# Prompt attention in four rounds: one program, projections between tiles, normalised probabilities, values as weights

## The chip, the cores and the metric

One core of a Trainium2 chip runs the whole program. The metric is the device time of one execution in microseconds (us). The engines are TensorE (PE in the profile, its weight loads PEld), VectorE (DVE), ScalarE (ACT), GpSimd (POOL) and SyncE (SP, which issues most DMAs). Each works through its own list of instructions in order; semaphores join them.

## What is computed

One step of a two-layer decoder. In each layer three mixers work on the same input: latent attention, a short convolution, and a recurrent mixer. The change concerns the attention of the 1024 prompt tokens, with 8 heads. In the reference:

```python
s = (jnp.einsum('bqhc,bkc->bhqk', q_lat, ckv).astype(jnp.float32)
     + jnp.einsum('bqhr,bkr->bhqk', q_pe, kpe).astype(jnp.float32)) * ATTN_SCALE
mask = k_pos[None, :] <= q_pos[:, None]
s = jnp.where(mask[None, None], s, -jnp.inf)
p = jax.nn.softmax(s, axis=-1).astype(ckv.dtype)
...
o_mla = jnp.einsum('bthc,chv->bthv', o_lat, p['w_uv']).reshape(B, T, D_MLA)
y_mla = (o_mla * jax.nn.silu(z_mla)) @ p['w_mla_out']
```

`q_lat` is the non-rotary part of the query (64 numbers a head) taken through `w_uk`, `q_pe` its rotary part (32 numbers), `ckv` the latent of 256 numbers a token. The kernel computes keys (ckv through w_uk) and values (ckv through w_uv) of each head instead, which gives the same sums. Everything is float32.

## The kernel before

`attention` (L2287 on) runs, for each layer, `prompt_attention` inside a hardware loop over four pairs of heads (the rounds), then the decoding stages for 64 sample tokens. Each call of `prompt_attention` is a phase: at its end the semaphores are cleared and all engines meet.

A round has three parts.

Projections. SP loads the round's columns of w_q_b in three pieces a head (L1756 to L1758), w_uk and w_uv. PE computes the queries of two heads in six groups of up to 364 tokens (L1770), ACT copies them to `q_t` (L1864), DVE applies the rotary factors to rows 64 to 95 of each head (L1902, L1903, L1905). PE computes keys (L1775; ACT copies, L1868) and values (L1779; DVE copies, L1908), turns w_uk (L1786) and computes the latent queries of the samples (L1795). POOL copies the rotary keys below the others (L1893).

Tiles. A tile is one block of 128 queries (`qt`, 0 to 7) of one head; it sees `(qt + 1) * 128` keys. The order is head by head: eight tiles of head 0, then eight of head 1. For each tile: scores on PE (L1808) into one of two banks of 1024 columns; on DVE the causal mask on the last 128 columns (L1919), the maximum (L1921) and its negative (L1923); on ACT the exponential with its row sum (L1884); on PE the transposes of the 128x128 blocks (L1817), on ACT their copies to `probs_t` (L1857); on PE the outputs, with the turned probabilities as 128-column weights and 64 columns of values streaming (L1827); on DVE the reciprocal of the sum (L1928) and the scaling of the 128x64 output (L1931).

End. The 128x128 results of the eight query blocks, two heads beside each other, are turned (L1846), and DVE multiplies them into `o_mla`, which holds the gate (L1944).

What sets the order of the work on PE is written out by hand:

```python
for a in range(n_jobs + 1):
    if a < n_jobs:
        pe.wait_ge(exped, a + 1)
        for f in range(len(fours[a])):
            turns(a, f)
    if a + 2 < n_jobs:
        scores(a + 2)
    if a:
        for f in range(len(fours[a - 1])):
            outputs(a - 1, f)
```

ACT does in turn the exponential of tile a and the copies of tile a - 1; DVE the maximum of tile a + 2 and the scaling of tile a - 1.

Two other places are named later. `page_attention` (the decoding stage) computes the values of two halves of a group in turn, with 64 columns of weights and output rows 0 to 63 or 64 to 127 (L2138), between transposes of full width (L2124) and scores (L2114). L723 is in the convolution.

## Time and profile before

| | |
|---|---|
| runs shown | 4146.57, 4148.21, 4152.67 us; median 4148.21 |
| the profiled execution | 4152.63 us, span of its instructions 4150.2 us |
| mean granted TensorE clock | 0.92 of full speed |
| PE busy | 3670.6 us (88% of the span), 28472 matmul instructions |
| PE weight loads busy | 2433.3 us (59%) |
| DVE busy | 1620.1 us (39%) |
| ACT busy | 888.2 us (21%) |
| POOL busy | 263.3 us (6%) |
| largest groups | L842 (gates, 787.9 us), L498 (projections), L2114, L2138, L2408 |

Busy times of PE are modelled ends of pipelined matmuls and overlap; a share of the whole span is a mean over stages with different limits. Prompt attention lies at about 1160 to 1468 us in layer 0 and 3195 to 3502 us in layer 1.

### The profile page before, as it was taken

To read this page: it belongs to the slowest core of one execution; us is meant where nothing else is said; L and a number is where in the kernel's file an instruction comes from. 1 tells how busy PE (TensorE), PEld (TensorE's weight loads), DVE (VectorE), ACT (ScalarE), POOL (GpSimd) and SP (SyncE) were. 2 spreads that over 40 slices of the span, in tenths; PEclk is the share of its full clock that TensorE was granted. 3 is DMA by queue.
4 is the path that set the end of the run, shared out by engine and by line. 5 is a ranking of instruction groups with operands and counts; after the bars stand their busy time and mean duration, and the time that the engine had idled before them with its cause. 6 is when DMAs were issued, how large, how long until landed. Compare 5 with 4: busy or idle time off the path is not lost. (4 is left out here: it accounts for less than half of the span.)

```text
span 4150.2 us, 67196 instructions
## 1 busy us (share of the span) xinstructions
PE 3670.6 (88%) x28472; PEld 2433.3 (59%) x28472; DVE 1620.1 (39%) x3054; ACT 888.2 (21%) x1778; POOL 263.3 (6%) x285
## 2 busy tenths in 40 slices
PE   5989989999778879989979899899995888899996
PEld 3555656666456657755536555566663665676654
DVE  3021024544344558844122010344433444777422
ACT  1110012222133422221022000222211443222201
POOL 0000000000000024400000000000000000442000
PEclk9999989999688979989979999999995998899998
DMA  7210111111000047734251110211110000775433
GB/s 269 51 38 16 46 43 53 50 51 54 13 18 7 6 166 271 274 115 138 74 192 25 51 33 16 64 47 53 56 41 16 7 6 7 275 263 202 149 119 121
DMA packets 282621, 362.89 MB, mean 87 GB/s; under 512 B 57188, under 2 KB 234294, under 8 KB 265832
## 3 DMA queue, kind: packets, MB, share of 16 engines
q1 hardware_dynamic: 244640, 190.00, 15.3%
q0 software_dynamic: 25808, 155.47, 10.1%
q10 hardware_dynamic: 11896, 13.44, 0.9%
q8 instruction: 210, 3.44, 0.3%
q14 instruction: 67, 0.55, 0.0%
HBM read 310.50 MB, written 48.35 MB: 86 GB/s over the span
## 5 line engine op out<-in xcount | busy, mean ns | idle before, releaser
L842 PE MATMUL rwkv_gate_bank<-u,rwkv_gate_w 128*128 128x364 f32 (+1 forms) x2304 | 787.9, 485 | 8.7 <-DMA rwkv_wa<-in_rwkv_a_dram 8.7
L842 PEld LDWEIGHTS rwkv_gate_bank<-u,rwkv_gate_w 128*128 128x128 f32 x2304 | 421.1, 192 | 232.1 <-issue 11.1
L498 PE MATMUL mla_b<-u,mla_w 128*128 128x364 f32 (+1 forms) x960 | 297.7, 473 | 27.6 <-DMA mla_w<-in_w_in_dram 27.6
L2173 DVE STREAM_TRANSPOSE u<-dec_ckv 128x2048 f32<-128x2048 f32 x112 | 258.5, 2308 | 52.9 <-DMA dec_ckv<-in_cache_mla_ckv_dram,dec_page_row 52.9
L2114 PE MATMUL dec_s_bank<-u,att_q_rows 32*64 32x256 f32 x8192 | 244.6, 386 | 32.6 <-DVE kpe L2176 32.6
L498 PE MATMUL rwp_b<-u,rwp_w 128*128 128x364 f32 (+1 forms) x864 | 267.0, 473 | 3.6 <-DMA rwp_w<-in_w_in_dram 3.6
L498 PEld LDWEIGHTS mla_b<-u,mla_w 128*128 128x128 f32 x960 | 184.7, 193 | 139.0 <-DMA mla_w<-in_w_in_dram 27.8
L2408 PE MATMUL out_b<-merged,out_w 128*128 128x364 f32 (+1 forms) x768 | 239.9, 477 | 13.0 <-DMA out_w<-in_w_out_dram 13.0
L498 PE MATMUL conv_b<-u,conv_w 128*128 128x364 f32 (+1 forms) x768 | 238.8, 475 | 4.9 <-DMA conv_w<-in_w_in_dram 4.9
L2138 PE MATMUL dec_o_bank<-dec_ckv,cq 128*64 128x256 f32 x1792 | 234.9, 382 | 7.7 <-DVE att_o_all L2199 6.5
L2114 PEld LDWEIGHTS dec_s_bank<-u,att_q_rows 32*64 32x64 f32 x8192 | 185.8, 135 | 74.4 <-DVE kpe L2176 39.8
L498 PEld LDWEIGHTS rwp_b<-u,rwp_w 128*128 128x128 f32 x864 | 166.0, 192 | 103.6 <-DMA rwp_w<-in_w_in_dram 3.8
L2408 PEld LDWEIGHTS out_b<-merged,out_w 128*128 128x128 f32 x768 | 148.8, 194 | 104.1 <-DMA out_w<-in_w_out_dram 14.2
L1893 POOL COPY attn_k_t<-kpe 32x1024 f32<-32x1024 f32 x16 | 16.1, 1032 | 3036.7 <-POOLq L171 3036.7
L856 ACT ACTIVATE rwkv_gate_stage<-rwkv_gate_bank 128x364 f32<-128x364 f32 x144 | 67.7, 470 | 648.2 <-PE rwkv_gate_bank L842 647.6
L498 PEld LDWEIGHTS conv_b<-u,conv_w 128*128 128x128 f32 x768 | 148.3, 193 | 94.5 <-DMA conv_w<-in_w_in_dram 5.1
L2138 PEld LDWEIGHTS dec_o_bank<-dec_ckv,cq 128*64 128x64 f32 x1792 | 145.8, 137 | 87.8 <-issue 32.7
L1808 PE MATMUL attn_s<-attn_k_t,attn_q_t 96*128 96x512 f32 (+3 forms) x384 | 160.9, 534 | 6.8 <-ACT att_q_lat L1876 6.8
L1827 PEld LDWEIGHTS attn_b<-attn_v,attn_probs_t 128*128 128x128 f32 x1152 | 146.9, 194 | 27.4 <-issue 19.7
L1770 PE MATMUL attn_s<-cq,attn_wq 128*128 128x364 f32 (+1 forms) x288 | 106.7, 537 | 62.4 <-DMA attn_wq<-in_w_q_b_dram 62.4
L2157 ACT ACTIVATE ckv<-dec_s_bank,dec_minus_top 128x1024 f32<-128x1024 f32 x64 | 71.3, 1114 | 370.7 <-DVE dec_minus_top L2185 370.7
L1827 PE MATMUL attn_b<-attn_v,attn_probs_t 128*128 128x64 f32 x1152 | 143.3, 271 | 0.0
(470 smaller groups left out, 4716.7 us busy)
## 6 DMA issues: line engine op xcount, KB each, us to landing
merge_sig<-gates_feature_major SPq DMA_DIRECT2D x16, 1632.0 KB, 8.8
mod_w<-in_w_ada_dram SPq DMA_DIRECT2D x12, 2048.0 KB, 13.6
rwkv_gate_w<-in_w_in_dram SPq DMA_DIRECT2D x48, 512.0 KB, 4.0
gates_feature_major<-rwkv_gate_stage SPq DMA_DIRECT2D x96, 182.0 KB, 1.9
mla_w<-in_w_in_dram SPq DMA_DIRECT2D x18, 512.0 KB, 3.8
rwp_w<-in_w_in_dram SPq DMA_DIRECT2D x18, 512.0 KB, 4.0
u<-x_feature_major SPq DMA_DIRECT2D x8, 1088.0 KB, 14.3
out_x<-x_feature_major SPq DMA_DIRECT2D x16, 544.0 KB, 4.3
```

The source lines that it names most:

```text
L498: mm = pe.matmul(self.banks[j % len(self.banks)][:, 0:m], self.w[:, n % self.NW, k, :], s.u[:, k, t0:t0 + m], start=(k == 0), stop=(k == K ...
L842: mm = pe.matmul(self.banks[j % 2][:, 0:m], self.w[:, n % GATE_CHUNKS, k, :], self.s.u[:, k, t0:t0 + m], start=(k == 0), stop=(k == KD - 1))
L856: act.activation(self.stage[j % 3][:, 0:m], self.banks[j % 2][:, 0:m], ACT.Copy).then_inc(self.emptied, 1)
L1770: mm = pe.matmul(B01[j % 2][:, 0:m], wq[:, k, i, :], s.cq[:, k, t0:t0 + m], start=(k == 0), stop=(k == 2))
L1808: mm = pe.matmul(B01[a % 2][:, c:c + n], q_t[i][0:QK, qt * P:(qt + 1) * P], k_t[i][0:QK, c:c + n], start=True, stop=True)
L1827: mm = pe.matmul(out_b[a % 2][:, 0:VH], probs_t[:, j % 4, x * P:(x + 1) * P], v[:, kt, i * VH:(i + 1) * VH], start=(kt == 0), stop=(kt == qt))
L1893: pool.tensor_copy(k_t[i][64:96, :], s.kpe[64:96, 0:SEQ]).then_inc(kpe_copied, 1)
L2114: mm = pe.matmul(S[64 * half:64 * half + NQ, 512 * i:512 * i + NK], q, keys, start=(cb == 0), stop=(cb == BLOCKS))
L2138: mm = pe.matmul(O[64 * half:64 * half + NQ, 0:KV_LORA], probs_t[:, j * P + 64 * half:j * P + 64 * half + NQ], ckv[(2 * a + half) % NS][:, ...
L2157: act.activation(probs.rearrange("p (j i k) -> p i j k", j=KEYS, i=4), s_view.rearrange("p i (j k) -> p i j k", j=KEYS), ACT.Exp, scale=AT ...
L2173: dve.transpose(kt[o % NT].rearrange("p (c j k) -> p j c k", c=BLOCKS, j=KEYS), ckv[o % NS].rearrange("p (j c k) -> p j c k", c=BLOCKS, j= ...
L2408: mm = pe.matmul(banks[j % NB][:, 0:m], w[:, n % NW, k, :], merged[:, k, t0:t0 + m], start=(k == 0), stop=(k == KD - 1))
```

## The change

`prompt_attention` is called once a layer, without the loop. It runs 64 tiles in one phase, `(round, query block, head)`, so that the two heads of a round alternate. The first round's projections stand ahead of the tiles; those of round r + 1 are cut into twelve pieces, which stand behind tiles 0 to 9 of round r (two each behind tiles 0 and 1). All projections and all transposed blocks go through one ring of two banks, written by PE and emptied by ACT; so ACT now copies the values too. Weights, keys, queries and values are doubled; the queries and keys lie in `s.u`, which is free in this stage. The rotary operations of the next round stand one by one behind tiles 3 to 10 on DVE.

DVE now divides by the row sum before the transposes: it scales the probabilities, up to 128x1024, in place (L1956 of the changed kernel). The outputs are computed once for both heads of a query block, two tiles later (L1845): 64 columns of values are the weights, 128 columns of turned probabilities stream, head 0 writes partitions 0 to 63 and head 1 partitions 64 to 127 of the same bank. The result is already turned: the transposes of L1846 go, and DVE multiplies 512 columns into `o_mla` (L1962) after each four query blocks.

```diff
-    NT = SEQ // P
+def prompt_attention(nc, s, l, q_lat, q_pe):
...
+    NT, NP = SEQ // P, HEADS // 2
...
-    tiles = [(i, qt) for i in range(2) for qt in range(NT)]
-    n_jobs = len(tiles)
-    fours = [[range(k, min(k + 4, qt + 1)) for k in range(0, qt + 1, 4)] for _, qt in tiles]
-    before = [sum(len(f) for f in fours[:a]) for a in range(n_jobs + 1)]
+    tiles = [(r, qt, i) for r in range(NP) for qt in range(NT) for i in range(2)]
+    qg = [(i, g) for i in range(2) for g in range(NG)]
+    pieces = [("q", x) for x in range(6)] + [("k", 0), ("k", 1), ("v", 0), ("v", 1), ("uk", 0), ("lat", 0)]
+    after_tile = {0: 2, 1: 2, 2: 1, 3: 1, 4: 1, 5: 1, 6: 1, 7: 1, 8: 1, 9: 1}
+    blocks = lambda a: [range(k, min(k + 4, tiles[a][1] + 1)) for k in range(0, tiles[a][1] + 1, 4)]
+
+    ring, pieces_at = [(0, *p) for p in pieces], {}
+    for a, (r, qt, i) in enumerate(tiles):
+        ring += [("turn", a, f) for f in range(len(blocks(a)))]
+        first = sum(after_tile.get(x, 0) for x in range(a % 16))
+        pieces_at[a] = [(r + 1, *p) for p in pieces[first:first + after_tile.get(a % 16, 0)]] if r + 1 < NP else []
+        ring += pieces_at[a]
+    slot = {job: j for j, job in enumerate(ring)}
...
-        wq = ph.sb("wq", [P, 3, 2, P])
-        wuk, wuv = ph.sb("wuk", [P, 2, P]), ph.sb("wuv", [P, 2, P])
+        wq = [ph.sb(f"wq{i}", [P, 3, 2, P]) for i in range(2)]
...
-        q_t = [ph.sb(f"q_t{i}", [P, T]) for i in range(2)]
-        k_t = [ph.sb(f"k_t{i}", [P, SEQ]) for i in range(2)]
+        q_t = [[s.u[:, 2 * x + i, :] for i in range(2)] for x in range(2)]
+        k_t = [[s.u[:, 4 + 2 * x + i, 0:SEQ] for i in range(2)] for x in range(2)]
...
-        v = ph.sb("v", [P, NT, P])
-        probs = ph.sb("probs", [P, 2, SEQ])
-        probs_t = ph.sb("probs_t", [P, 4, 512])
...
-        o = ph.sb("o", [P, NT, P])
-        B = [ph.bank(f"s{i}", (P, 1024)) for i in range(2)] + [ph.bank(f"b{i}") for i in range(4)]
-        B01, turn, out_b = B[0:2], B[2:4], B[4:6]
...
+        S = [ph.bank(f"s{i}", (P, 1024)) for i in range(2)]
+        R = [ph.bank(f"ring{i}") for i in range(2)]
+        O = [ph.bank(f"o{i}") for i in range(2)]
...
+                for r in range(NP):
+                    x = r % 2
+                    if r >= 2:
+                        sp.wait_ge(ring_written, slot[(r - 2, "lat", 0)] + 1)
...
+                def ring_bank(job):
+                    j = slot[job]
                     if j >= 2:
-                        pe.wait_ge(q_read, j - 1)
-                    for k in range(3):
...
-                def turns(a, f):
-                    j = before[a] + f
-                    if j >= 2:
-                        pe.wait_ge(copied, j - 1)
-                    for x, kt in enumerate(fours[a][f]):
-                        mm = pe.transpose(turn[j % 2][:, x * P:(x + 1) * P], probs[:, a % 2, kt * P:(kt + 1) * P], s.tab["ident"])
-                    mm.then_inc(turned, 1)
-
-                def outputs(a, f):
-                    i, qt = tiles[a]
-                    j = before[a] + f
-                    pe.wait_ge(copied, j + 1)
-                    if f == 0 and a >= 2:
-                        pe.wait_ge(read, a - 1)
-                    for x, kt in enumerate(fours[a][f]):
-                        mm = pe.matmul(out_b[a % 2][:, 0:VH], probs_t[:, j % 4, x * P:(x + 1) * P],
-                                       v[:, kt, i * VH:(i + 1) * VH], start=(kt == 0), stop=(kt == qt))
+                def turns(a):
+                    pe.wait_ge(normed, a + 1)
+                    for f, four in enumerate(blocks(a)):
+                        bank = ring_bank(("turn", a, f))
+                        for x, kt in enumerate(four):
+                            mm = pe.transpose(bank[:, x * P:(x + 1) * P], probs[a % 2][:, kt * P:(kt + 1) * P], ident)
+                        mm.then_inc(ring_written, 1)
+
+                def outputs(a):
+                    r, qt, _ = tiles[a]
+                    pair = a // 2
+                    if qt == 0:
+                        pe.wait_ge(ring_read, slot[(r, "v", 1)] + 1)
+                    if qt % 4 == 0 and pair >= NT:
+                        pe.wait_ge(evicted, 2 * (pair // NT - 1) + qt // 4 + 1)
+                    pe.wait_ge(ring_read, slot[("turn", a + 1, len(blocks(a + 1)) - 1)] + 1)
+                    for kt in range(qt + 1):
+                        for i in range(2):
+                            mm = pe.matmul(O[qt // 4][VH * i:VH * (i + 1), qt % 4 * P:(qt % 4 + 1) * P], v[r % 2][:, kt, VH * i:VH * (i + 1)],
+                                           probs_t[:, pair % 2, i, kt * P:(kt + 1) * P], start=(kt == 0), stop=(kt == qt))
                     mm.then_inc(summed, 1)
...
+                for p in pieces:
+                    prologue(0, *p)
                 scores(0)
                 scores(1)
...
+                for a in range(len(tiles)):
+                    turns(a)
+                    if a + 2 < len(tiles):
                         scores(a + 2)
-                    if a:
-                        for f in range(len(fours[a - 1])):
-                            outputs(a - 1, f)
...
+                    if a >= 2 and a % 2 == 0:
+                        outputs(a - 2)
+                    for p in pieces_at[a]:
+                        prologue(*p)
+                outputs(len(tiles) - 2)
...
+                def exponential(a):
+                    n = (tiles[a][1] + 1) * P
                     act.wait_ge(topped, a + 1)
                     if a >= 2:
...
+                        act.wait_ge(ring_written, slot[("turn", a - 2, len(blocks(a - 2)) - 1)] + 1)
+                    act.activation(probs[a % 2][:, 0:n], S[a % 2][:, 0:n], ACT.Exp, scale=ATTN_SCALE,
                                    bias=minus_top[:, a:a + 1], accum_out=total[:, a:a + 1]).then_inc(exped, 1)
-                    if a:
-                        copies(act, a - 1)
-                copies(act, n_jobs - 1)
+
+                def keep_turned(a):
+                    _, qt, i = tiles[a]
+                    for f, four in enumerate(blocks(a)):
+                        j = slot[("turn", a, f)]
+                        n = len(four) * P
+                        act.wait_ge(ring_written, j + 1)
+                        act.activation(probs_t[:, a // 2 % 2, i, 4 * f * P:4 * f * P + n], R[j % 2][:, 0:n], ACT.Copy).then_inc(ring_read, 1)
+
+                for p in pieces:
+                    keep(0, *p)
+                exponential(0)
+                for a in range(len(tiles)):
+                    if a + 1 < len(tiles):
+                        exponential(a + 1)
+                    keep_turned(a)
+                    for p in pieces_at[a]:
+                        keep(*p)
...
+                def rope(r, step):
+                    i, n = divmod(step, 4)
+                    q = q_t[r % 2][i]
+                    if n == 0:
+                        dve.wait_ge(ring_read, slot[(r, "q", 3 * i + 2)] + 1)
+                        if r or i:
+                            dve.wait_ge(roped, 6 * r + 3 * i)
+                        dve.tensor_tensor(swapped[64:96, :], q[96:128, :], sin, ALU.mult).then_inc(roped, 1)
+                    elif n == 1:
+                        dve.tensor_tensor(q[64:96, :], q[64:96, :], cos, ALU.mult).then_inc(roped, 1)
+                    elif n == 2:
+                        dve.wait_ge(roped, 6 * r + 3 * i + 2)
+                        dve.tensor_tensor(q[64:96, :], q[64:96, :], swapped[64:96, :], ALU.add).then_inc(roped, 1)
+                    else:
+                        dve.wait_ge(roped, 6 * r + 3 * i + 3)
+                        dve.tensor_copy(q_pe[64:96, :, 2 * r + i, :], q[64:96, SEQ:T].rearrange("p (b t) -> p b t", t=STEPS)).then_inc(q_pe_kept, 1)
...
-                def finish(a):
-                    i, qt = tiles[a]
+                def normalise(a):
+                    n = (tiles[a][1] + 1) * P
                     dve.wait_ge(exped, a + 1)
                     dve.reciprocal(inv_total[:, a:a + 1], total[:, a:a + 1]).then_inc(inverted, 1)
                     dve.wait_ge(inverted, a + 1)
-                    dve.wait_ge(summed, before[a + 1])
-                    dve.tensor_scalar(o[:, qt, i * VH:(i + 1) * VH], out_b[a % 2][:, 0:VH],
-                                      inv_total[:, a:a + 1], None, ALU.mult).then_inc(read, 1)
-
+                    dve.tensor_scalar(probs[a % 2][:, 0:n], probs[a % 2][:, 0:n], inv_total[:, a:a + 1], None, ALU.mult).then_inc(normed, 1)
+
+                def evict(n):
+                    r, h = divmod(n, 2)
+                    dve.wait_ge(summed, 8 * r + 4 * h + 4)
+                    out = s.o_mla[:, r, 512 * h:512 * (h + 1)]
+                    dve.tensor_tensor(out, out, O[h][:], ALU.mult).then_inc(evicted, 1)
...
+                for step in range(8):
+                    rope(0, step)
                 tops(0)
                 tops(1)
-                for a in range(n_jobs + 1):
-                    if a + 2 < n_jobs:
+                for a in range(len(tiles)):
+                    r, qt, i = tiles[a]
+                    normalise(a)
+                    if a + 2 < len(tiles):
                         tops(a + 2)
-                    if a:
...
+                    if r + 1 < NP and 3 <= a % 16 < 11:
+                        rope(r + 1, a % 16 - 3)
+                    if a % 16 == 9:
+                        evict(2 * r)
+                    elif r and a % 16 == 1:
+                        evict(2 * r - 1)
+                evict(2 * NP - 1)
...
-        with nc.Fori(0, HEADS // 2) as hp:
-            prompt_attention(nc, s, l, hp, q_lat, q_pe)
+        prompt_attention(nc, s, l, q_lat, q_pe)
```

How PE's instructions move: from tile 2's transposes on, before (`attn_s` holds scores, `attn_b` are the banks of transposes and outputs; the first number of the shape is the columns of weights or rows of output, the last the columns streamed):

```order
L1817 MATMUL attn_b<-tables,attn_probs 128x128 x3
L1808 MATMUL attn_s<-attn_k_t,attn_q_t 128x512
L1808 MATMUL attn_s<-attn_k_t,attn_q_t 128x128
L1827 MATMUL attn_b<-attn_v,attn_probs_t 128x64 x2
L1817 MATMUL attn_b<-tables,attn_probs 128x128 x4
L1808 MATMUL attn_s<-attn_k_t,attn_q_t 128x512
L1808 MATMUL attn_s<-attn_k_t,attn_q_t 128x256
L1827 MATMUL attn_b<-attn_v,attn_probs_t 128x64 x3
```

The same engine, tiles 4 and 5 of the first round, changed (`attn_ring` is the ring, `u` holds queries and keys, `attn_o` the output banks):

```order
L1832 MATMUL attn_ring<-tables,attn_probs 128x128 x3
L1823 MATMUL attn_s<-u 128x512
L1845 MATMUL attn_o<-attn_probs_t,attn_v 64x128 x4
L1792 MATMUL attn_ring<-ckv,attn_wuk 128x512 x2
L1832 MATMUL attn_ring<-tables,attn_probs 128x128 x3
L1823 MATMUL attn_s<-u 128x512
L1792 MATMUL attn_ring<-ckv,attn_wuk 128x512 x2
L1832 MATMUL attn_ring<-tables,attn_probs 128x128 x4
```

Outputs now come every second tile, for both heads, and the keys' projections of the next round (L1792) stand between the tiles.

On DVE, one tile before:

```order
L1928 RECIPROCAL attn_inv_total<-attn_total 128x1
L1931 TENSOR_SCALAR attn_o<-attn_b,attn_inv_total 128x64
L1919 TENSOR_TENSOR attn_s<-attn_s,tables 128x128
L1921 TENSOR_REDUCE attn_top<-attn_s 128x1
L1923 TENSOR_SCALAR attn_minus_top<-attn_top 128x1
```

And changed, tile 9 of the first round and what follows up to tile 10's scaling:

```order
L1954 RECIPROCAL attn_inv_total<-attn_total 128x1
L1956 TENSOR_SCALAR attn_probs<-attn_probs,attn_inv_total 128x640
L1945 TENSOR_TENSOR attn_s<-attn_s,tables 128x128
L1947 TENSOR_REDUCE attn_top<-attn_s 128x1
L1949 TENSOR_SCALAR attn_minus_top<-attn_top 128x1
L1936 TENSOR_TENSOR u<-u,attn_swapped 32x1088
L1962 TENSOR_TENSOR o_mla<-o_mla,attn_o 128x512
L1954 RECIPROCAL attn_inv_total<-attn_total 128x1
L1956 TENSOR_SCALAR attn_probs<-attn_probs,attn_inv_total 128x768
```

The scaling now stands ahead of the transposes and is 640 columns wide here instead of 64; a rotary operation and the product stand ahead of the next tile's scaling.

## Rows read from the trace of the kernel before

**Rows 1.** Windows by stage; window, length, busy us of each engine, clock, DMA, GB/s

```profile
1166.70:1189.60 22.90, 21.40 (x88) 14.21 (x88) 9.37 (x10) 6.37 (x15) 0.00 (x0) 0.93 0.09 20
1189.60:1234.70 45.10, 42.64 (x265) 33.47 (x265) 24.86 (x80) 22.75 (x56) 0.00 (x0) 0.92 0.00 1
1234.70:1242.50 7.80, 1.08 (x8) 0.84 (x8) 1.28 (x2) 1.28 (x1) 2.02 (x2) 0.73 0.17 30
1239.39:1315.59 76.20, 65.51 (x360) 48.44 (x360) 35.52 (x92) 30.41 (x73) 2.00 (x3) 0.90 0.04 9
1166.70:1465.50 298.80, 261.89 (x1440) 194.38 (x1440) 142.06 (x368) 120.34 (x287) 6.05 (x6) 0.91 0.04 8
3201.00:3499.90 298.90, 261.81 (x1440) 194.35 (x1440) 142.10 (x368) 120.34 (x287) 6.05 (x6) 0.91 0.04 8
```

**Rows 2.** Windows, in the first tiles and at the second round's first projections

```profile
1192.00:1194.00 2.00, 2.00 (x5) 1.06 (x5) 0.66 (x2) 0.59 (x3) 0.00 (x0) 0.50 0.00 0
1243.00:1247.00 4.00, 4.00 (x8) 2.11 (x8) 0.00 (x0) 0.40 (x1) 0.00 (x0) 0.50 0.37 82
```

**Rows 3.** Timeline across a round's end; start us, us, engine, line, [idle before <-releaser]

```profile
1235.49 1.28 DVE L1944 TENSOR_TENSOR o_mla<-o_mla,attn_b 128x512 f32 x2 [0.86 <-PE attn_b L1846]
...
1239.39 0.38 SPq L1756 DMA_DIRECT2D attn_wq<-in_w_q_b_dram  x1
...
1242.55 0.98 PE L1770 MATMUL attn_s<-cq,attn_wq 128*128 128x364 f32 x1 [6.78 <-DMA attn_wq<-in_w_q_b_dram]
```

**Rows 4.** Timeline of the first round: runs of equal instructions on PE and PEld

```profile
1169.91 9.08 PEld L1770 LDWEIGHTS attn_s<-cq,attn_wq 128*128 128x128 f32 x30 [0.27 <-issue]
1182.84 3.73 PE L1779 MATMUL attn_b<-attn_wuv,ckv 128*128 128x128 f32 x32
1187.69 1.10 PE L1795 MATMUL attn_b<-attn_q_t,attn_wuk_t 64*128 64x64 f32 x8 [0.68 <-ACT attn_wuk_t L1871]
1204.13 1.88 PE L1808 MATMUL attn_s<-attn_k_t,attn_q_t 96*128 96x512 f32 x4
1206.91 0.93 PE L1817 MATMUL attn_b<-tables,attn_probs 128*128 128x128 f32 x7
1230.67 3.43 PEld L1827 LDWEIGHTS attn_b<-attn_v,attn_probs_t 128*128 128x128 f32 x30
```

**Rows 5.** Timeline, the chain of the first 1024-column tile and the start of the next, of 128 columns

```profile
1206.05 0.30 DVE L1919 TENSOR_TENSOR attn_s<-attn_s,tables 128x128 f32<-128x128 f32 x1 [1.22 <-PE attn_s L1808]
1206.38 1.23 DVE L1921 TENSOR_REDUCE attn_top<-attn_s 128x1 f32<-128x1024 f32 x1
1207.83 1.11 ACT L1884 ACTIVATE attn_probs<-attn_s,attn_minus_top 128x1024 f32<-128x1024 f32 x1 [1.50 <-DVE attn_minus_top L1923]
1208.61 0.29 DVE L1921 TENSOR_REDUCE attn_top<-attn_s 128x1 f32<-128x128 f32 x1
1209.00 0.15 DVE L1928 RECIPROCAL attn_inv_total<-attn_total 128x1 f32<-128x1 f32 x1
1209.79 0.38 ACT L1884 ACTIVATE attn_probs<-attn_s,attn_minus_top 128x128 f32<-128x128 f32 x1
```

**Rows 6.** Groups by line and form: count, busy us, mean ns, idle before

```profile
L723 DVE TENSOR_SCALAR conv_y<-conv_past_p,vecs 128x1024 f32<-128x1024 f32 x4 | 2.8, 748 | 0.0
L723 DVE TENSOR_SCALAR conv_y<-conv_past_s,vecs 128x64 f32<-128x64 f32 x4 | 0.8, 249 | 0.0
L1902 DVE TENSOR_TENSOR attn_swapped<-attn_q_t,tables 32x1088 f32<-32x1088 f32 x16 | 20.6, 1287 | 134.8 <-ACT attn_q_t L1864 134.8
L1944 DVE TENSOR_TENSOR o_mla<-o_mla,attn_b 128x512 f32 x16 | 10.3, 683 | 6.9 <-PE attn_b L1846 6.9
```

**Rows 7.** Timeline in the decoding stage, PE: halves side by side, then full-width transposes

```profile
1707.36 3.67 PE L2138 MATMUL dec_o_bank<-dec_ckv,cq 128*64 128x256 f32 x32
1710.96 1.09 PE L2124 MATMUL dec_pt_bank<-tables,ckv 128*128 128x128 f32 x8
1711.98 3.71 PE L2114 MATMUL dec_s_bank<-u,att_q_rows 32*64 32x256 f32 x128
```

208 lines of the change are left out of this document (86 added, 122 removed).

## The prediction

> **What bounds the kernel now.** I read the windows by stage first, because the change touches one stage only, prompt attention, which runs once in each of the two layers. From the first projection matmul to the last product it takes 298.8 us in the first layer and 298.9 us in the second [rows 1], together 598 of 4150 us. Nothing else in the program is edited, so the sum is made over these two stretches. Look at two things in rows 1. PE is busy for 262 of 298.8 us, while DVE has 142 and ACT 120: TensorE is the bound, and a change of DVE or ACT work is worth nothing unless it ends up in TensorE's way. And the four rounds repeat: a round is 76.2 us, of which the projections take 22.9 us, the 16 tiles 45.1 us and the gap between rounds 7.8 us with 1 us of PE work in it.
>
> Next the granted clock: it is 0.50, that is 1.2 GHz, in the first microseconds of the tiles, behind a stretch in which PE mostly waited, and again at the start of the next round's projections behind the gap [rows 2]. So a gap costs twice, once as idle time and once as slow matmuls after it.
>
> Then the timeline across the end of a round, to see what the 7.8 us are: the last products on DVE, the end of the phase (semaphores cleared, all engines meet), and then PE idle for 6.8 us until the weights have come, whose first load SP issues only at 1239.39 [rows 3].
>
> Last the pace of TensorE's instructions at full clock [rows 4]. The "busy" durations overlap, so I divide the length of a run of equal instructions by their number. Each float32 matmul stands twice in the profile. Projection of 364 columns: 9.08/30 = 0.303 us each. Values, 128 columns: 3.73/32 = 0.117. Scores: (1.88 - 0.17)/4 = 0.427 for 512 columns, where 0.17 is the tail of the last one, so 0.834 ns a column; the keys have the same form. Transposes, one instruction each: about 0.115. The probability-times-value matmuls (L1827) stream only 64 columns, yet take 3.43/30 = 0.114: they go at the pace of their 128-column weight loads.
>
> **The sum, round by round, before.** Projections: 36 x 0.303 = 10.9, keys 8 x 0.427 = 3.4, values 32 x 0.117 = 3.7, the turned w_uk and the sample latents 1.6 (the latter 1.1 in rows 4): 19.6 us. Scores: 9216 columns, twice, x 0.834 ns = 15.4. Transposes 72 x 0.115 = 8.3. Outputs 144 x 0.114 = 16.4. The eight transposes of the result 0.9. That is 60.6 of 76.2 us; the other 15.6 us are the gap (6.8), slow clock, and waits at the seams and between small tiles.
>
> **Part 1, one program of four rounds.** The loop and three of four phase ends go. The weights of the next round are loaded a round ahead, so SP's DMA issues no longer stand before PE. Gone per layer: three gaps of 7.8 us and the slow projections after them. The first round's 22.9 us [rows 1] stay, and I add 0.5 us since all its results now pass through two banks and ACT takes the values' copies as well.
>
> **Part 2, projections between tiles.** They are not hidden: PE is the bound, so their 19.6 us are paid in full. What they fill are the waits of the small tiles. ACT, busy for 30 of 76 us a round [rows 1], takes 1.4 us of values' copies more and stays hidden. The rotary work on DVE is not quite: three operations of 1.29 us for each head [rows 6], one behind each of tiles 3, 4, 5, 7, 8 and 9. DVE then has for tile 8 (768 columns reduced, 640 scaled): mask 0.33, reduce 0.96 (between 0.29 for 128 and 1.23 for 1024, rows 5), two small ones 0.30, multiply 0.55, rotary 1.29, together 3.4 us, and for tile 9 a product of 0.68 more [rows 6], 4.1 us. PE has 0.6 of transposes, 1.3 of scores, 0.6 of outputs and 0.45 of w_uk: 2.9 us. I take 3 us a round of waiting for DVE; bounds are 0 (the slack of two tiles absorbs it) and 7.7 (all six operations in PE's way).
>
> **Part 3, normalised probabilities.** Was: 128x64 scaled after the output. Now: the reciprocal and a multiply over up to 1024 columns stand before the transposes. No such multiply of attn_probs exists yet; the nearest, DVE TENSOR_SCALAR from and to SBUF by a per-row number, takes 748 ns at 1024 columns and 249 ns at 64 [rows 6], so 0.22 + 0.52n/1000, some 8 us of DVE a round, where DVE had 35.5 of 76. The chain that matters is from the end of a tile's scores to its transposes. For 1024 columns: the scores' streaming ends at about 1205.84; mask at 1206.05, reduce 1.23, exponential 1.11, reciprocal at 1209.00 [rows 5]; plus 0.15, the multiply 0.75 and a hop of 0.1: 4.2 us. PE has between the two, by the new order, one outputs call, the other tile's transposes and scores: 1.9 + 0.3 + 0.9 + 1.7 = 4.8 us. Hidden, by 0.6 us. For 128 columns the reduce and the exponential fall to 0.29 and 0.38 [rows 5] and the multiply to about 0.3, so the chain is 2.0 us, while PE has 0.9 us: a hole of 1.1 us per pair, then about 0.9, 0.6 and 0.4 for 256, 384 and 512 columns, 3 us together. In rounds 1 to 3 the pieces fill these; in the last round nothing does.
>
> **Part 4, values as weights, two heads side by side.** The 144 outputs now load 64 columns of weights and stream 128 columns; the two heads write partitions 0 to 63 and 64 to 127 of one bank, in turn. The trace of before has this form in the decoding stage with 256 columns: 32 instructions in 3.67 us [rows 7], 0.113 us each, where 256 columns alone would take 256 x 0.834 = 0.213. So two halves do run at once. For 128 columns the bounds are 0.053 (half of 107 ns) and 0.115 (no overlap, like L1827). I take 0.06, since rows 7 stand 6 ns above half: 144 x 0.06 = 8.6 us instead of 16.4. The result comes out turned already, so 0.9 us of transposes go.
>
> Against this stands the change of shape. Behind the halves the next eight full-width transposes take 1.02 us from their first start to the start of what follows (1710.96 to 1711.98), 0.128 each instead of 0.107 to 0.115 [rows 7], 0.1 to 0.17 us for a change. There are two changes per outputs call, 16 a round: at 0.16, 2.6 us a round, 21 us over both layers; bounds 0 and 0.3. The Trainium skill (TensorEngine Tiling (Array Packing), Key Properties) says that changing the tiling mode, unlike changing only the tile, drains TensorE. It is the rule against this change; by rows 7 the drain is short, and without it the forecast would be 21 us lower.
>
> **Sum per layer.** A round with next projections: 19.6 + 15.4 + 8.3 + 8.6 + 2.6 = 54.5, plus 3 = 57.5 us, three times: 172.5. Last round: 34.9 + 3 of holes + 2.8 at its end (the last tile's normalising is exposed by 1.4, then copy and product) = 40.7. First projections 23.4. Slow clock in the first tiles, as in rows 2, and once more in the thin tiles of the last round: 5. Total 241.6, against 298.8: 57.2 less, 114.5 for both layers. The profiled execution took 4152.6 us around its span of 4150.2; the median of the runs shown is 4148.2, 4.4 lower. On the median: **4034 us**. A measurement of this kernel can tell about 0.2% (8 us) from no change.
>
> **The rivals.**
> *A. The heads do not overlap at 128 columns*, because the weight loads of both halves share one path. For it: L1827 shows loads setting the pace. Against: rows 7. Outputs then cost 0.115: 7.9 us more a round, of which some 2 were waiting anyway: 24 a layer, **4082**.
> *B. DVE binds.* The rotary operations are all in the way (7.7 instead of 3) and PE waits some 2 us a round more at the two ring banks while ACT copies keys (two copies of 0.6 us). 7 us in three rounds, 21 a layer: **4076**. For it: DVE is in order and each tile needs it twice. Against: its work is some 38 us in 57 (35.5 now [rows 1], less the 128x64 scalings and the values' copies, about 6, plus 8).
> *C. Slower: weights exposed.* Inside each head's strip the load cannot go under the running matmul and the strips take turns: 0.11 + 0.115 = 0.225 an instruction, 24 us more a round. Less the 8 us of waits that this covers, 87 a layer against 57 gained: 60 us slower, **4208**. It turns the sign from 0.173 us an instruction on (65/576 above 0.06). Rows 7 show 0.113 for twice the columns, so this is unlikely.
> That the change does not do what it says can only mean that the gaps stay inside the tiles; that is B.
>
> **How the numbers follow.** Forecast 0.64, A 0.17, B 0.14, C 0.03, anything else 0.02. The low bounds together (0.053, no change of shape, no DVE waits, no slow clock) are 28 us a layer, 3977; all at once is unlikely, so the range starts at 3995 and ends above A, at 4090. Faster 0.96, same 0.01, slower 0.03.
>
> **What would show it.** In the changed profile: each stretch near 242 us; no PE gap of several us inside it; L1845 at 0.055 to 0.07 us an instruction (A: 0.11); TensorE's clock at full level from the second round on; DVE as releaser of the transposes for a few us a round (B: over 7). The sum is wrong if PE's idle time in the tiles grows, or if L1832 and L1823 after L1845 start more than 0.3 us late.

## The result: 1.9% slower

The changed kernel takes **4228.7 us** (median of 4 runs, 4224.8 to 4233.6) against 4149.7 us of the kernel before (4 runs). The ratio is **1.0191, 95% interval 1.0173 to 1.0209**: slower by 79 us, where 114 us less was forecast. It lies above the range of 3995 to 4090.

### The profile after

First the stage in whole, by windows: the two stretches from the first projection matmul to the last product on DVE, then, of layer 0, the first projections and the four rounds, cut where the first transpose of each starts. The columns are those of [rows 1].

```profile
1167.60:1504.70 337.10, 254.15 (x1408) 162.39 (x1408) 154.72 (x360) 123.70 (x285) 0.00 (x0) 0.89 0.03 7
3238.00:3580.10 342.10, 261.71 (x1408) 166.58 (x1408) 154.76 (x360) 123.93 (x285) 0.00 (x0) 0.86 0.03 7
1167.60:1190.00 22.40, 21.53 (x88) 14.29 (x88) 8.07 (x8) 6.87 (x13) 0.00 (x0) 0.91 0.18 41
1192.90:1272.70 79.80, 59.72 (x320) 38.21 (x320) 38.22 (x89) 30.25 (x71) 0.00 (x0) 0.92 0.07 15
1272.70:1352.90 80.20, 61.79 (x352) 39.22 (x352) 38.82 (x90) 30.41 (x72) 0.00 (x0) 0.91 0.00 1
1352.90:1433.00 80.10, 60.96 (x352) 39.42 (x352) 38.80 (x90) 30.13 (x72) 0.00 (x0) 0.91 0.00 1
1433.00:1504.70 71.70, 49.40 (x292) 30.74 (x292) 28.96 (x76) 23.51 (x54) 0.00 (x0) 0.79 0.00 1
```

The stretches are 337.1 and 342.1 us against 298.8 and 298.9 [rows 1]: 38.3 + 43.2 = 81.5 us more, which covers the whole difference of 79 us. PE has less work than before, and in the first layer it is busy for 254 us, not 262; but it now stands idle for 83 us of the stretch, not 37. Two things are striking. The first projections take 22.4 us, about as forecast. And a round takes 80 us, more than before, gap and all, and the last one 71.7 us, although it has no next projections in it and 19.6 us less work on PE: a round's length no longer follows PE's work. (Part of the 71.7 us is the clock, which is lower in the last round, 0.79 against 0.91.)

Next who waits for whom, in layer 0 (1167 to 1505 us): us in total, times, longest. Then the two groups of the whole page in which those waits stand.

```profile
DVE attn_s L1945 <- PE attn_s L1823: 156.9, 63, 5.2
PEld attn_ring L1832 <- DVE attn_probs L1956: 102.6, 48, 3.5
PE attn_ring L1832 <- DVE attn_probs L1956: 80.4, 47, 3.3
ACT attn_probs L1893 <- DVE attn_minus_top L1949: 73.5, 32, 4.4
...
PE attn_o L1845 <- ACT attn_probs_t L1902: 0.7, 1, 0.7
```

```profile
L1832 PE MATMUL attn_ring<-tables,attn_probs 128*128 128x128 f32 x576 | 103.1, 313 | 158.5 <-DVE attn_probs L1956 158.3
L1945 DVE TENSOR_TENSOR attn_s<-attn_s,tables 128x128 f32<-128x128 f32 x128 | 38.3, 299 | 318.2 <-PE attn_s L1823 318.2
```

Read the first and third line together. PE's transposes (L1832) wait for DVE's scaling 80.4 us, in 47 of 64 tiles. And DVE's mask (L1945), the head of the maximum, waits for PE's scores 156.9 us, in 63 of 64. Neither engine is full, and each waits for the other about once a tile. That is the sign of a loop. The tiles without such a wait on PE are 1, 2, 3, 7 and 15 of the first three rounds and 1 and 15 of the last; in tiles 1, 2, 3 and 7 PE has projections of the next round to do meanwhile. PE's wait for ACT, which empties the ring of two banks, is 0.7 us in the tiles (last line), so the ring is not what holds it up.

The timeline shows one lap of it (start us, us, engine, line; in brackets the idle time before and who ended it):

```profile
1254.00 1.01 ACT L1893 ACTIVATE attn_probs<-attn_s,attn_minus_top 128x896 f32<-128x896 f32 x1 [2.50 <-DVE attn_minus_top L1949]
...
1254.82 0.98 PE L1832 MATMUL attn_ring<-tables,attn_probs 128*128 128x128 f32 x7 [2.50 <-DVE attn_probs L1956]
...
1255.64 1.88 PE L1823 MATMUL attn_s<-u 96*128 96x512 f32 x4
...
1257.45 1.53 PE L1845 MATMUL attn_o<-attn_probs_t,attn_v 128*64 128x128 f32 x24
1257.56 0.30 DVE L1945 TENSOR_TENSOR attn_s<-attn_s,tables 128x128 f32<-128x128 f32 x1 [2.80 <-PE attn_s L1823]
1257.89 1.22 DVE L1947 TENSOR_REDUCE attn_top<-attn_s 128x1 f32<-128x1024 f32 x1
1259.15 0.15 DVE L1949 TENSOR_SCALAR attn_minus_top<-attn_top 128x1 f32<-128x1 f32 x1
1259.22 0.15 DVE L1954 RECIPROCAL attn_inv_total<-attn_total 128x1 f32<-128x1 f32 x1
1259.34 1.12 ACT L1893 ACTIVATE attn_probs<-attn_s,attn_minus_top 128x1024 f32<-128x1024 f32 x1 [2.85 <-DVE attn_minus_top L1949]
1259.41 0.69 DVE L1956 TENSOR_SCALAR attn_probs<-attn_probs,attn_inv_total 128x896 f32<-128x896 f32 x1
1260.15 0.98 PE L1832 MATMUL attn_ring<-tables,attn_probs 128*128 128x128 f32 x7 [1.17 <-DVE attn_probs L1956]
...
1265.55 1.09 PE L1832 MATMUL attn_ring<-tables,attn_probs 128*128 128x128 f32 x8 [2.70 <-DVE attn_probs L1956]
```

From the transposes of one tile (12) to those of the next (13), at 1254.82 and 1260.15: transposes 0.82, scores 1.92, mask 0.33, maximum 1.26, its negative 0.07, reciprocal 0.19, scaling 0.74, together **5.33 us, and one tile further**. Nothing in it overlaps anything else in it. PE's own work in the same lap is 0.8 + 1.9 + 1.3 = 4.0 us, and in the laps of odd tiles, without outputs, 2.7. A round of 80 us is 16 laps of 5.0 us in the mean, the last one 16 of 4.5. (The last line above is the transposes of tile 14; they are used further down.)

**Theory L (the loop).** DVE does in order: scale a, find the maximum of a + 2, scale a + 1. PE does in order: transposes of a, scores of a + 2. So scale a → transposes a → scores a + 2 → maximum a + 2 → scale a + 1. The last step is no need of the data: the exponential of a + 1 was ready long before (in the lap shown it ended at 1255.01, its reciprocal started at 1259.22). It is DVE's list alone that puts scaling a + 1 behind a maximum whose scores wait for scaling a. In the kernel before the transposes waited for the exponential only; the way round (exponential a → transposes a → scores a + 2 → maximum a + 2 → exponential a + 2) led two tiles on.

**Rivals.** N: the DVE work of the scaling itself is too much (any order would be slow). D: DVE binds through the rotary operations (B of the prediction). O: the outputs side by side, or what is around them, cost more than was thought (A and C of the prediction).

### The profile page after: what moved, and what is told of

It is laid out like the page before. It is cut to its first block and busy times, and to the rows that moved or that the text cites. A ratio compares the mean times of both kernels' runs of the same rounds, so it can differ in the third digit from the quotient of the medians.

```text
span 4227.1 us, 66254 instructions
## 1 busy us (share of the span) xinstructions
PE 3652.9 (86%) x28408; PEld 2364.3 (56%) x28408; DVE 1644.5 (39%) x3038; ACT 892.4 (21%) x1772; POOL 255.1 (6%) x277
## 5 line engine op out<-in xcount | busy, mean ns | idle before, releaser
L1832 PE MATMUL attn_ring<-tables,attn_probs 128*128 128x128 f32 x576 | 103.1, 313 | 158.5 <-DVE attn_probs L1956 158.3
L1832 PEld LDWEIGHTS attn_ring<-tables,attn_probs 128*128 128x128 f32 x576 | 72.2, 157 | 209.3 <-DVE attn_probs L1956 203.2
L1823 PE MATMUL attn_s<-u 96*128 96x512 f32 (+3 forms) x384 | 176.2, 575 | 0.0
L2125 POOL DMA_INDIRECT dec_ckv<-in_cache_mla_ckv_dram,dec_page_row x112 | 105.8, 944 | 999.0 <-DVE dec_page_row L2237 733.4
L1945 DVE TENSOR_TENSOR attn_s<-attn_s,tables 128x128 f32<-128x128 f32 x128 | 38.3, 299 | 318.2 <-PE attn_s L1823 318.2
```

Source lines behind the costliest of these rows:

```text
L1823: mm = pe.matmul(S[a % 2][:, c:c + n], q_t[r % 2][i][0:QK, qt * P:(qt + 1) * P], k_t[r % 2][i][0:QK, c:c + n], start=True, stop=True)
L1832: mm = pe.transpose(bank[:, x * P:(x + 1) * P], probs[a % 2][:, kt * P:(kt + 1) * P], ident)
L1945: dve.tensor_tensor(d, d, s.tab["causal"], ALU.add).then_inc(masked, 1)
L2125: pool.indirect_dma_start(ckv[o % NS], None, ckv_rows, rows).then_inc(c_in[o % NS], 16)
```

## The experiments

The kernels were run in three groups of four (e1 to e4, e5 to e8, e9 to e12), each beside runs of the kernel before. That takes 4146.8 us (7 runs) in the first group, 4432.4 (10 runs) in the second and 4150.2 (15 runs) in the third. The 285 us more of the second group lie outside prompt attention, as far as the traces of e7 and e8 can tell (last section), so its kernels are compared by their difference to before and by the length of the stretch; the times expected of them were worked out from 4150 us and are read the same way.

### e1: scores ahead of transposes

```diff
                 for a in range(len(tiles)):
-                    turns(a)
                     if a + 2 < len(tiles):
                         scores(a + 2)
+                    turns(a)
```

> PE issues the scores of tile a+2 ahead of the transposes of tile a; nothing else changes. Theory L (a loop of one tile: scaling of a, transposes of a, scores of a+2, maximum of a+2, scaling of a+1, because DVE and PE work in order): the scores leave the loop, a lap spans two tiles, and PE binds again in the large tiles. PE's waits for the scaling fall from 158 us to under 50, the time to 4040 to 4080 us. Theory D (DVE has too much work, above all the rotary operations): DVE's work is the same, so the time stays at 4210 to 4230. Theory C (the chain from the scores' end to the transposes, 4 to 5 us, is too long for two tiles in flight): a part comes back, as the scores start earlier, 4150 to 4190.

Measured: 4044.5 us (4041.4 to 4050.8), ratio **0.9743 [0.9727, 0.9759]**. Two lines swapped on PE turn 79 us of loss into 102 us of gain. The windows of rounds 0 to 2 and the whole stretch:

```profile
1190.00:1248.00 58.00, 53.27 (x291) 33.89 (x292) 38.39 (x92) 30.20 (x72) 0.00 (x0) 0.97 0.11 23
1248.00:1306.00 58.00, 55.02 (x348) 35.96 (x345) 37.77 (x88) 29.35 (x71) 0.00 (x0) 1.00 0.00 1
1306.00:1364.00 58.00, 55.47 (x351) 36.24 (x349) 37.74 (x89) 29.12 (x70) 0.00 (x0) 1.00 0.00 1
1166.90:1413.00 246.10, 227.45 (x1408) 148.71 (x1408) 153.39 (x360) 122.17 (x285) 0.00 (x0) 0.98 0.05 10
```

The windows are 58 us long and PE is busy for 55 of them from the second on; counted from first transpose to first transpose (1251.25, 1310.09, 1368.93) a round is 58.8 us. TensorE's clock is at full level from the second round on. DVE does the same 153 us of work as in the changed kernel (154.7): the work was never the trouble. In place of 80.4 us the transposes wait 11.9 us for the scaling in layer 0:

```profile
PE attn_ring L1832 <- DVE attn_probs L1956: 11.9, 15, 1.9
```

### e2: no scaling

The multiplication of the probabilities by the reciprocal is left out (the output is not normalised), and the transposes wait for the exponential. PE's and DVE's orders are those of the changed kernel.

```diff
-                    pe.wait_ge(normed, a + 1)
+                    pe.wait_ge(exped, a + 1)
...
-                    dve.wait_ge(inverted, a + 1)
-                    dve.tensor_scalar(probs[a % 2][:, 0:n], ...).then_inc(normed, 1)
```

> The multiplication of the probabilities by the reciprocal of their sum is left out; the transposes wait for the exponential alone. Theory L: DVE's scaling no longer releases the transposes, the loop is gone: 4020 to 4060 us. Theory D: only the 66 us of multiplications over both layers go, at most: 4165 or more. Theory C: the chain is shorter by the multiplication, the reciprocal and their hops, about 1 us in each of 64 laps of two tiles, about 4150.

Measured: 4020.3 us, ratio 0.969 [0.9673, 0.9706]. Against 1.0191 the scaling in its place costs 5 points; against e1 (0.9743) it costs half a point. So it is its place in the loop that costs, hardly its time. (e1 and e2 differ in PE's order too; e12 finds that order worth 0.1% in the kernel before.)

### e3: scaling ahead of the maximum

```diff
                 tops(1)
+                normalise(0)
                 for a in range(len(tiles)):
...
-                    normalise(a)
+                    if a + 1 < len(tiles):
+                        normalise(a + 1)
                     if a + 2 < len(tiles):
                         tops(a + 2)
```

> DVE does the scaling of tile a+1 ahead of the maximum of tile a+2 instead of behind it. Theory L: the loop is cut at another place, but DVE now waits for the exponential between a maximum and the scaling of the same tile (1.3 us of 4.1 a large tile, partly under the rotary operations): 4060 to 4110 us. Theory D: no change, 4210 to 4230. Theory C: no change or slower, since DVE stands still for the exponential.

Measured: 4053.9 us, ratio 0.9765 [0.9749, 0.9781], some 6 us better than the lower end expected. PE's order is that of the changed kernel here, transposes first; only DVE's list is changed. That the loop opens from either side is the strongest sign for L: a cost of TensorE (O) would not go by an edit of DVE's list, and all of DVE's work (N) is still there.

### e4: the heads one after the other

e1, with the outputs of head 0 all ahead of those of head 1, in place of one of each in turn.

```diff
-                    for kt in range(qt + 1):
-                        for i in range(2):
+                    for i in range(2):
+                        for kt in range(qt + 1):
```

> As e1_scores_first, but the outputs of head 0 all stand before those of head 1, so the two halves of the array no longer alternate. If TensorE binds after e1, this adds (0.107 - 0.055) x 1152 = 60 us, or 30 to 60 with waits absorbed. If another chain still binds in e1, it adds under 15 us. The instructions' own pace shows whether alternating is what makes the halves overlap: 0.11 us each against 0.055.

Measured: 4087.1 us, ratio 0.9849 [0.9833, 0.9866], 43 us more than e1, inside the 30 to 60 expected. The runs of equal outputs on PE, first in e1, then in e4:

```profile
1226.12 1.09 PE L1845 MATMUL attn_o<-attn_probs_t,attn_v 128*64 128x128 f32 x16
...
1239.71 0.98 PE L1832 MATMUL attn_ring<-tables,attn_probs 128*128 128x128 f32 x7
1240.62 1.53 PE L1845 MATMUL attn_o<-attn_probs_t,attn_v 128*64 128x128 f32 x24
1242.08 1.98 PE L1823 MATMUL attn_s<-u 96*128 96x512 f32 x4
```

```profile
1253.07 2.89 PE L1845 MATMUL attn_o<-attn_probs_t,attn_v 128*64 128x128 f32 x28
...
1257.99 3.33 PE L1845 MATMUL attn_o<-attn_probs_t,attn_v 128*64 128x128 f32 x32
```

In e1 eight more instructions take 1.53 - 1.09 = 0.44 us, **0.055 each**; in e4 four more take 3.33 - 2.89 = 0.44, **0.110 each**. The same instructions run at twice the pace if the halves alternate. 576 x 0.055 = 32 us a layer would be the full price; 43/2 = 22 show, the rest fell into waits. With O the changed kernel would owe its loss to these outputs; they run at 0.055 in it too (below).

### e5: the scaling alone, put into the kernel before

Nothing of the change but the scaling of the probabilities ahead of the transposes, in the changed kernel's order; the four phases a layer, the gaps and the outputs with 128-column weights stay.

```diff
-                        pe.wait_ge(exped, a + 1)
+                        pe.wait_ge(normed, a + 1)
...
-                for a in range(n_jobs + 1):
+                for a in range(n_jobs + 2):
+                    if a < n_jobs:
+                        normalise(a)
                     if a + 2 < n_jobs:
                         tops(a + 2)
-                    if a:
-                        finish(a - 1)
+                    if a >= 2:
+                        finish(a - 2)
```

`normalise` is that of the changed kernel, and `finish` only copies.

> The kernel before with one part of the change alone: DVE scales the probabilities by the reciprocal ahead of the transposes (which wait for it), and only copies the outputs, of tile a-2, behind the maximum of tile a+2. The loop of four rounds, the old order of tiles and the old outputs stay. Theory L: the same one-tile loop appears in the old kernel, 4 to 5.3 us for a large tile against some 3.5; the 16 tiles of a round go from 45 to 60 to 66 us: 4270 to 4320 us. Theory N (the scaling is harmful only together with the projections and rotary operations between the tiles): under 4190.

Measured: 4763.5 us against 4432.4, ratio **1.0738 [1.072, 1.0756]**: 331 us more, where 120 to 170 more than before were expected. Right in sign, but twice the size: the clock was left out. A window from the first projections to just before the last products of layer 0, the waits for the scaling in that layer, and one lap:

```profile
1167.40:1628.90 461.50, 364.39 (x1428) 268.66 (x1429) 166.15 (x429) 127.84 (x287) 6.05 (x6) 0.67 0.02 5
```

```profile
PE attn_b L1818 <- DVE attn_probs L1931: 69.8, 48, 1.8
```

```profile
1218.87 1.15 PE L1818 MATMUL attn_b<-tables,attn_probs 128*128 128x128 f32 x6 [1.72 <-DVE attn_probs L1931]
...
1219.81 3.35 PE L1809 MATMUL attn_s<-attn_k_t,attn_q_t 96*128 96x512 f32 x4
...
1225.92 1.57 PE L1818 MATMUL attn_b<-tables,attn_probs 128*128 128x128 f32 x7 [1.70 <-DVE attn_probs L1931]
```

The stretch ends at 1633.2 and is 465.8 us long, 167 more than the 298.8 of [rows 1]; twice that, 334, is the whole difference of 331 us. The lap is 7.05 us, and the granted clock is 0.67 of full speed over the stretch, against 0.91 before: four scores take 3.35 us instead of 1.88. The waits for the scaling are 69.8 us, and the stretch is 167 us longer, so the loop costs twice. PE waits in 48 of 64 tiles, the clock is lower, and since transposes and scores are part of the lap, the lap grows, with the wait still in it.

### e6: the same, scores first

e5 with `scores(a + 2)` ahead of the wait for `normed` and of the transposes.

> As e5_scaling_alone, with the scores of tile a+2 ahead of the transposes of tile a on PE. Theory L: the loop is gone, DVE's 66 us of extra work lie mostly beside PE's: 4150 to 4190 us. Theory N: no change against e5.

Measured: 4448.0 against 4432.4, ratio 1.0033 [1.0022, 1.0045]: 16 us more than before, where 0 to 40 were expected. The same edit as e1 takes 7 points off. It ran in the same group as e5, and its stretch is 307.4 us at a mean clock of 0.92 (e5: 0.67), so the low clock came with the loop.

```profile
1166.70:1474.10 307.40, 265.55 (x1440) 193.06 (x1440) 166.60 (x432) 125.22 (x287) 6.05 (x6) 0.92 0.04 8
```

What is left, 16 us, is what the scaling costs this kernel in a good order.

### e7, e8: rotary operations on POOL

e7 is the changed kernel, e8 is e1, each with the rotary multiplications, sums and copies on POOL in place of DVE (same operations, `pool.` for `dve.`).

> The changed kernel with all rotary operations and the copies of q_pe on POOL instead of DVE; the order of PE and DVE as in the changed kernel. Theory L: the six rotary operations of a round lie in the loop with their full 1.29 us, less where PE's projections are longer than the lap (tile 3): 3 rounds x 2 layers x 6 x 1.29 = 46 us at most come off, some is given back in the first round if POOL is slower: 4185 to 4205 us. The large rest of the loss stays. Theory D: DVE's load was the bound, so most of the loss goes: under 4130.

> Scores first (as e1) and the rotary operations on POOL. With the loop cut, PE binds (55 of 58 us a round busy), so taking 8 us a round off DVE brings little: 4020 to 4045 us, against 4044 for e1. If POOL's slower operations hold up the first round, up to 10 us are given back: to 4055.

Measured: e7 4469.4 us, ratio 1.0084 [1.0067, 1.0101], 37 us more than before, where L expected 35 to 55 (the changed kernel: 79); e8 4323.9 us, ratio 0.9757 [0.9741, 0.9774], 108 us less than before (e1: 102), also as expected. In the changed kernel the operations lengthened some of the laps, and taking them away gives back half of the loss (the stretches are 318 and 322 us instead of 337 and 342), but it stays slower than before. Theory D had expected it under the time of before. With the loop open nothing is to be had: e8's stretches are 247 and 245 us, e1's 246 and 246. So D is a part of what fills the lap, and not the cause. On POOL one of these takes 2.48 us, against 1.29 on DVE [rows 6]; there is room for it.

### e9, e10, e11: what e1 still leaves

e9 is e1 with e3's order on DVE. e10 is e1 with the outputs ahead of the transposes:

```diff
                         scores(a + 2)
-                    turns(a)
                     if a >= 2 and a % 2 == 0:
                         outputs(a - 2)
+                    turns(a)
```

e11 is both.

> The changed kernel with both orders mended: PE issues the scores of tile a + 2 ahead of the transposes of tile a (as in e1), and DVE scales tile a + 1 ahead of the maximum of tile a + 2 (as in e3). Theory L (one lap of PE, DVE and ACT for each tile): e1 has opened the lap already, and 23.8 us of waiting for the scaling are left in both layers together, most of it where rotary operations stand ahead of the scaling on DVE. With the second order the scaling no longer stands behind a maximum, so some of these go: 0 to 15 us less than e1, a ratio to before of 0.970 to 0.975 (e1: 0.9743). Rival (the two orders block each other, since a DVE that waits for the exponential of tile a + 1 is late for the maximum of a + 2): above 0.978.

> The kernel e1 with the outputs of the last pair ahead of the transposes of tile a too, so PE has scores (up to 1.7 us) and outputs (up to 0.9 us) between the end of the exponential and the transposes that need the scaling. Theory L: some of the 23.8 us of waiting for the scaling are covered for every second tile: 3 to 12 us less than e1, a ratio to before of 0.971 to 0.974. Rival (ring and probs_t hold it: the outputs wait for ACT's copies of tile a - 1, and the wait only moves from L1832 to L1845): no change or worse, 0.974 to 0.977.

> e10 and e9 together: scores and outputs ahead of the transposes on PE, scaling ahead of the maximum on DVE. Theory L: if each takes a part of the 23.8 us that e1 still waits for the scaling, together up to 20 us less than e1, a ratio of 0.969 to 0.974. If the rest of the waits is not the scaling, all three kernels stand within 0.2% of e1.

Measured: e9 0.9754 [0.9741, 0.9768], **e10 4024.3 us, 0.9696 [0.9683, 0.9709]**, e11 0.9761 [0.9748, 0.9775]. e10 is the fastest kernel of the study: 126 us under before and 204 under the changed kernel. It gains more than the 3 to 12 us on e1 that were expected, some 20 us. e9 stands just above its range (0.970 to 0.975) and below its rival's 0.978, and e11 misses its range (0.969 to 0.974) altogether. The whole stretch and the waits from 1190 to 1500 us in e10:

```profile
1168.00:1404.60 236.60, 223.69 (x1408) 148.46 (x1408) 153.62 (x360) 121.77 (x285) 0.00 (x0) 0.98 0.05 10
```

```profile
PE attn_o L1845 <- ACT attn_probs_t L1902: 3.9, 8, 0.7
PE attn_s L1823 <- ACT attn_probs L1893: 2.0, 2, 1.8
PE attn_ring L1832 <- DVE attn_probs L1956: 0.8, 2, 0.4
```

The wait for the scaling falls from 11.9 to 0.8 us, and the outputs wait 3.9 us for ACT's copies, against 0.7 in e1: the rival expected of e10 is there, but small. e9 and e11 gain nothing on e1. DVE now waits for ACT ahead of the maximum, so the exponential of the tile after can only come later. The waits of e9 in the same stretch:

```profile
DVE attn_inv_total L1954 <- ACT attn_probs L1893: 67.7, 48, 6.4
...
PE attn_s L1823 <- ACT attn_probs L1893: 10.1, 14, 1.8
...
PE attn_ring L1832 <- DVE attn_probs L1956: 5.2, 8, 1.5
```

The scores wait 10.1 us for the exponential there, where e10 has 2.0 and e1 1.8; the transposes wait 5.2 us for the scaling, where e1 has 11.9. That is 15.3 us in all against 13.7. Two mends of this loop are not better than one; the second only moves the wait.

### e12: control, the kernel before with scores first

```diff
                         pe.wait_ge(exped, a + 1)
+                        if a + 2 < n_jobs:
+                            scores(a + 2)
                         for f in range(len(fours[a])):
                             turns(a, f)
-                    if a + 2 < n_jobs:
-                        scores(a + 2)
```

> Control: the kernel before with one part of e1's edit, the scores of tile a + 2 ahead of the transposes of tile a, both behind the wait for the exponential of tile a. Theory L says that the order of scores and transposes matters only where the transposes wait for something later than the scores do. In the kernel before both wait for the same exponential, so nothing is gained: 0.997 to 1.004. If the order of the two is worth something by itself (maxima found earlier, a steadier clock), before becomes 0.5% or more faster here, and part of e1's gain is no undoing of a loss of the change.

Measured: 0.9988 [0.9979, 0.9997], within what was expected. In that kernel the order by itself is worth 0.1%. With e1 and e6 beside it, the order matters once the transposes wait for something later than the scores do, and that was new with the scaling.

## Why the prediction was wrong

The step that failed is in **Part 3**: "PE has between the two, by the new order, one outputs call, the other tile's transposes and scores: 1.9 + 0.3 + 0.9 + 1.7 = 4.8 us. Hidden, by 0.6 us." The pieces of that chain had the right size: in the lap shown above, 3.1 us from the end of the scores of tile 14 (about 1257.35) to the end of its exponential (1260.46), and 0.93 for reciprocal and scaling of 896 columns (1259.22 to 1260.15). The cover was not there: the other tile's transposes need the other tile's scaling, and DVE issues that behind the maximum of the very tile whose chain was to be covered. So the 2.6 us of transposes and scores could not run beside the chain, but stood in line with it, and tile 14's own transposes start at 1265.55, 8.2 us after its scores end. The sum had 3 us a round for waits of PE on DVE; the changed kernel shows 80.4 / 4 = 20 us. I had laid DVE's work and PE's work side by side as sums and had not followed DVE's list one tile on. Only the outputs (half a call a tile) and the next projections lay beside the chain, and without the projections the last round is only 8 us shorter than the others, for 19.6 us less work, at a lower clock.

Its price by the trace: 337.1 - 246.1 (e1) = 91 us in layer 0, and e1 against the changed kernel 4.5 points in all. Of these, 68.5 us are waits for the scaling (80.4 - 11.9); and the same 1408 matmul instructions are busy for 254.2 instead of 227.5 us, at a mean clock of 0.89 instead of 0.98.

Point by point:

- *Part 1, gaps and slow clock.* The gaps of 6.8 us between the rounds are gone; the longest wait left on PE in layer 0 of the changed kernel is 3.3 us, and it is one for the scaling. The first projections end with the window at 1190.0, 22.4 us after 1167.6, against 22.9 + 0.5 forecast. The clock was forecast at full level from the second round on: in the changed kernel it is 0.91, 0.91 and 0.79, with the loop open (e1) it is full.
- *Part 2, projections between tiles, 3 us of DVE waits a round.* In e1, PE is busy for 55.0 and 55.5 of 58 us: 2.5 to 3 us idle. In the changed kernel it was 20 us, and the rotary work lengthened laps (e7).
- *Part 4, outputs at 0.06.* 0.055 in e1, and in the changed kernel too: its 24 outputs take 1.53 us, as in e1. The ends of the range were 0.053 and 0.115, and e4 shows the upper one as well, at 0.110.
- *Part 4, change of shape, 0.16.* In e1 seven transposes start at 1239.71, the outputs at 1240.62 and the scores at 1242.08. That is 0.91 - 7 x 0.115 = 0.10 for the one change and 1.46 - 24 x 0.055 = 0.14 for the other. The Trainium skill (TensorEngine Tiling (Array Packing), Key Properties) says that a change of mode drains TensorE; the trace agrees in that 0.10 to 0.14 us is lost each time.
- *The sum.* 57.5 us a round were forecast, 57.9 to 58.8 are measured in e1; 40.7 for the last round, against 44.1 (1368.93 to 1413.0); 241.6 for the layer, against 246.1 in e1 and 236.6 in e10. 4034 stands between e1's 4044 and e10's 4024. The terms of PE's work held, for kernels whose lists do not form the loop. That says nothing for the forecast of the changed kernel.
- *Rival A (heads do not overlap)*: refuted by 0.055. e4 shows when it would be true: 43 us, where A said 48.
- *Rival B (DVE binds)*: its sign came, DVE as releaser of the transposes for over 7 us a round (20 us), but it named the wrong thing: with the same work on DVE, e1 and e3 are 184 and 175 us faster. "DVE is in order and each tile needs it twice" was the right observation, and I then priced it by DVE's busy time, 38 of 57 us. The in-order lists bound here by the length of a way round (5.33 us a tile), not by busy time.
- *Rival C (weights exposed)*: refuted, 0.055 and not 0.225. The kernel is slower, as in C, and 4208 is the nearest number to 4228.7, but by another cause, so this is luck; no case of mine had it, and the 0.03 for "slower" was far too low. That the transposes had got a second wait in DVE's list should have given a rival of its own.

## What to carry to other kernels

When a change adds a step on one engine between two of another, follow the chain through both engines' lists until it comes back to the same step, and count how many tiles further it has come. The length of that way, divided by the tiles it advances, is a floor under the time per tile, whatever the busy times say (5.33 us for a tile here, where PE's own work is 2.7 to 4.0 us); two engines that both wait once a tile for each other in the waits view are its sign. One reordering was enough to open this loop (work that waits for less goes ahead of work that waits for more); afterwards the wait that was left was best filled with work that is already ready, which e10 does with the outputs.

## What the runs showed that was not expected

- A loop at low occupancy took the clock with it: 0.67 over e5's stretch, 0.86 and 0.89 in the changed kernel's (0.79 in its last round), 0.98 in e1's, with nearly the same instructions on PE as in the changed kernel. In e5 the waits of up to 1.8 us a tile add up to 69.8 us in layer 0, and the stretch is 167 us longer: they cost more than their own length.
- Two halves of the PE array, 64 columns of weights each, run 128-column float32 matmuls at 0.055 us an instruction in alternation and at 0.110 one half after the other (e1, e4).
- In the second group the kernel before took 4432 us, 7% more than in the others; no trace of it was taken there. In the traces of e5 to e8 the rate of the DMA in the decoding slices is lower. First the changed kernel, which was not in that group, then e7, which was (GB/s in 40 slices of the span; look at slices 15 to 18):

```profile
GB/s 264 50 37 36 25 46 52 56 51 45 14 26 1 1 142 269 267 133 136 73 192 20 52 31 28 54 54 51 52 35 25 7 1 1 242 272 209 150 112 124
```

```profile
GB/s 263 34 44 30 21 61 55 52 50 25 24 7 1 109 178 179 175 110 137 78 182 19 49 38 37 51 50 56 47 15 25 1 1 170 171 178 164 123 123 120
```

It is 175 to 179 GB/s where the changed kernel has 267 to 269. Prompt attention moves little by DMA and shows nothing of it: a window of 58 us of e8 holds 54.9 us of PE work, as in e1, and its stretches are 247 and 245 us. Why the rate was lower in that group stays open; no run was made for it.
